# Neighbourhood attention: each score tile as two products of 64 rows instead of one product padded to 128 rows

## The reference, cut to what matters

```python
def neighbourhood_latent(q, k, v, kc, vc, rpb):
    # per grid row r of queries, all heads
    s_loc = einsum('bqhd,bkhd->bhqk', qr, kr) * scale + bias     # 512 latent keys
    s_loc = where(mask, s_loc, -inf)                             # column window of 16
    s_ctx = einsum('bqhd,blhd->bhql', qr, kc) * scale            # 256 context keys
    p = softmax(concatenate([s_loc, s_ctx], -1), -1)
    return p_loc @ vr + p_ctx @ vc

def c_mixer(u, uc, in_w, out_w, rpb):
    q, k, v, z = split(u @ in_w, 4);  q_c, k_c, v_c, z_c = split(uc @ in_w, 4)
    return (neighbourhood_latent(q, k, v, k_c, v_c, rpb) * silu(z)) @ out_w
```

## Time and profile before

| | |
|---|---|
| time, median of 3 runs | 3423.76 us (3420.49 to 3424.57) |
| time of the profiled execution | 3419.06 us |
| its span, first to last instruction | 3417.3 us |
| PE busy | 2899.0 us, 85% |
| DVE, ACT, POOL busy | 833.0, 634.0, 200.3 us |
| mean granted clock of TensorE | 0.939 of full speed |
| attention `na0`, first scores after the bias tables to the next stage's first product | 3004.28 to 3096.57 us |
| attention `na1`, the same | 3276.74 to 3369.75 us |

### The profile page before, as it was taken

One profiled execution on the slowest core, in us unless ns is written; L12 is line 12 of the kernel. 1 busy time (PEld: TensorE's weight loads), 2 busy tenths in 40 slices (PEclk: granted clock), 3 DMA queues, 4 the chain that ended last, 5 costly groups with the idle time before them and its releaser, 6 DMA issues. The chain is left out here.

```text
span 3417.3 us, 30687 instructions
## 1 busy us (share of the span) xinstructions
PE 2899.0 (85%) x12394; PEld 1448.9 (42%) x12394; DVE 833.0 (24%) x2143; ACT 634.0 (19%) x1356; POOL 200.3 (6%) x148
## 2 busy tenths in 40 slices
PE   7999948877768999997688787489999997989987
PEld 3454532222224444444222222256566554455554
DVE  1130421110112212203111101315515351062054
ACT  2220310000001000001000000214414142051043
POOL 1000010000000000000000000200100110021021
PEclk9999969999988999998799999799999998999999
DMA  5502069999984242325699999510010101121010
GB/s 189 220 26 74 25 256 382 411 411 411 411 322 173 98 148 74 117 79 225 259 411 411 411 411 411 214 43 15 1 38 26 39 24 49 54 64 47 28 44 31
DMA packets 191103, 604.84 MB, mean 177 GB/s; under 512 B 9429, under 2 KB 23706, under 8 KB 190826
## 3 DMA queue, kind: packets, MB, share of 16 engines
q1 hardware_dynamic: 165360, 537.15, 40.6%
q10 hardware_dynamic: 20346, 46.88, 4.0%
q0 software_dynamic: 5248, 18.75, 1.5%
HBM read 559.16 MB, written 43.52 MB: 176 GB/s over the span
## 5 line engine op out<-in xcount | busy, mean ns | idle before, releaser
L477 PE MATMUL psum<-ring,XT 128*128 128x512 f32 (+3 forms) x1216 | 480.2, 555 | 14.1 <-ACT arena L1703 6.6
L467 PE MATMUL psum<-XT,ring 128*128 128x512 f32 (+1 forms) x1152 | 444.2, 547 | 2.8 <-DVEq L2053 2.8
L1059 PE MATMUL psum<-arena 128*64 128x512 f32 x1280 | 334.4, 673 | 116.2 <-DMA arena<-in_expert_w_gu 115.9
L477 PEld LDWEIGHTS psum<-ring,XT 128*128 128x128 f32 x1216 | 230.4, 191 | 255.5 <-issue 221.6
L467 PEld LDWEIGHTS psum<-XT,ring 128*128 128x128 f32 x1152 | 219.5, 191 | 226.5 <-issue 215.4
L559 PE MATMUL psum<-ring,arena 128*128 128x512 f32 x704 | 307.8, 596 | 8.5 <-DVEq L2053 4.2
L684 PE MATMUL psum<-arena 128*128 128x512 f32 (+8 forms) x704 | 258.3, 482 | 41.2 <-ACT arena L738 36.1
L1059 PE MATMUL psum<-ring,arena 128*64 128x512 f32 x768 | 199.5, 669 | 75.8 <-DMA ring<-in_expert_w_gu 72.9
L1059 PEld LDWEIGHTS psum<-arena 128*64 128x64 f32 x1280 | 98.7, 153 | 325.5 <-issue 197.8
L1129 DVE TENSOR_TENSOR arena<-arena,psum 64x512 f32<-64x512 f32 x64 | 44.2, 690 | 736.6 <-ACT arena L1132 736.6
L559 PEld LDWEIGHTS psum<-ring,arena 128*128 128x128 f32 x704 | 133.0, 191 | 172.8 <-issue 160.3
(11 more groups left out here) (243 smaller groups left out, 2286.8 us busy)
## 6 DMA issues: line engine op xcount, KB each, us to landing
arena<-in_expert_w_gu SPq DMA_DIRECT2D x80, 2048.0 KB, 25.5
ring<-in_expert_w_gu SPq DMA_DIRECT2D x48, 2048.0 KB, 26.0
arena<-in_expert_w_down SPq DMA_DIRECT2D x40, 2048.0 KB, 24.6
ring<-in_expert_w_down SPq DMA_DIRECT2D x24, 2048.0 KB, 26.0
ring<-in_ada_w SPq DMA_DIRECT2D x12, 2048.0 KB, 8.8
ring<-in_fox_w_in SPq DMA_DIRECT2D x8, 2048.0 KB, 8.3
arena<-xg_dram ACTq DMA_DIRECT2D x32, 512.0 KB, 6.8
y_dram<-arena ACTq DMA_DIRECT2D x128, 128.0 KB, 6.0
```

Of the source, the lines that this page charges most:

```text
L467: i = pe.matmul(ps[0][0:cols_[1] - cols_[0], 0:ntok], w[:, c, cols_[0]:cols_[1]], x[:, c, tok:tok + ntok], start=(c == 0), stop=(c == k - 1))
L477: i = pe.matmul(ps[0][:, 0:width], x[:, c, t * P:(t + 1) * P], w[:, c, c0:c0 + width], start=(c == 0), stop=(c == k - 1))
L1059: i = pe.matmul(psum[side * BR:(side + 1) * BR, 0:FF], x[:, 4 * part + c, :], w[:, c, side * FF:(side + 1) * FF], start=(part == 0 and c = ...
```

## The change

Q is now stored in both halves of the partitions: for each head the same 64 rows stand in partitions 0 to 63 and again in 64 to 127, and no zeros are needed. K is stored per head (`KT` has 8 heads of 384 columns in place of 4 pairs of 768): keys 0 to 383 in partitions 0 to 63, keys 384 to 767 (the last 128 latent keys and the 256 context keys) in partitions 64 to 127. A unit's scores are two products over 64 partitions, each of 384 keys, the one on the upper and the other on the lower half of the array's rows. They write PSUM columns 128 to 511 of the slot's first bank and 0 to 383 of its second, so that each has a bank of its own and the 768 scores are contiguous; all readers are moved by 128 columns (`P`), and the latent part that DVE reads now lies over both banks.

```diff
-                m, x = sm[:, 0, n:n + 1], self.s_at(n, 0, SEQ)
-                dve_step.then(dve, dve.tensor_reduce(m, self.s_at(n, SEQ, SEQ + CTX), AXX, ALU.max))
+                m, x = sm[:, 0, n:n + 1], self.s_at(n, P, P + SEQ)
+                dve_step.then(dve, dve.tensor_reduce(m, self.s_at(n, P + SEQ, P + SEQ + CTX), AXX, ALU.max))
...
-                QT, KT = region(6144, 2, 4, SEQ), region(10240, 4, NTA * P)
+                QT, KT = region(6144, 2, 4, SEQ), region(10240, 8, NTA // 2 * P)
...
-                zeros(p, *(QT[(1 - hh) * DH:(2 - hh) * DH, hh] for hh in range(2)))
...
                         for hh in range(2):
-                            r = slice(hh * DH, (hh + 1) * DH)
-                            i = dve.tensor_scalar(QT[r, hh, n, :], ps[0][r, :], DH ** -0.5, None, ALU.mult)
+                            for half in (slice(0, DH), slice(DH, P)):
+                                i = dve.tensor_scalar(QT[half, hh, n, :], ps[0][hh * DH:(hh + 1) * DH, :], DH ** -0.5, None, ALU.mult)
...
-                    tok_T(p, us[1], 0, KC, 512, (n * P, n * P + P), XT, KT[:, n, :], lambda d: copy_out("a", d), "a", True, n == 3)
+                    def latent_keys(act, ps, n=n, KT=KT):
+                        for hh in range(2):
+                            r = slice(hh * DH, (hh + 1) * DH)
+                            act.activation(KT[0:DH, 2 * n + hh, :], ps[0][r, 0:3 * P], ACT.Copy)
+                            i = act.activation(KT[DH:P, 2 * n + hh, 0:P], ps[0][r, 3 * P:SEQ], ACT.Copy)
+                        return i
+
+                    def context_keys(act, ps, n=n, KT=KT):
+                        for hh in range(2):
+                            i = act.activation(KT[DH:P, 2 * n + hh, P:3 * P], ps[0][hh * DH:(hh + 1) * DH, 0:CTX], ACT.Copy)
+                        return i
+                    p.job("a", mm_T(us[1], 0, KC, 512, (n * P, n * P + P), XT, 0, SEQ), latent_keys, units=(us[1],))
+                    p.job("a", mm_T(us[1], 0, KC, 512, (n * P, n * P + P), XT, SEQ, CTX), context_keys, units=(us[1],),
+                          release=(1,) if n == 3 else ())
...
-                    return [(0, SEQ, q, KT[:, h // 2, 0:SEQ]), (SEQ, SEQ + CTX, q, KT[:, h // 2, SEQ:SEQ + CTX])]
-                a = Neighbours(f"na{g}", 8, NT, lambda i: (0, 768), scores,
+                    return [(P, 4 * P, q[0:DH], KT[0:DH, h, :]), (4 * P, 7 * P, q[DH:P], KT[DH:P, h, :])]
+                a = Neighbours(f"na{g}", 8, NT, lambda i: (P, P + 768), scores,
```

## The result

| | before | after |
|---|---|---|
| time, median of 5 runs | 3423.76 us (3420.49 to 3424.57) | 3404.58 us (3401.82 to 3409.90) |
| ratio, 95% interval | | 0.9945 (0.9934 to 0.9957) |
| profiled execution, its span | 3419.06, 3417.3 us | 3406.55, 3404.8 us |
| na0, first scores to the next stage's first product | 108.29 us | 98.46 us |
| na1, the same | 104.28 us | 93.73 us |

The kernel is 19.2 us faster, 0.55%, where 19 were forecast. The spans of the two profiled executions differ by 12.5 us only, because in the second one everything up to mixer C came 8 us later. The kernel is the same up to there; in the ten traces (the two kernels and the eight experiments) mixer C begins between 2847.3 and 2855.5 us. Of the 8 us, 7 stand already in front of the first expert product (495.5 us before, 502.5 after); their cause was not looked into.

What follows compares the result with a forecast made beforehand. PE (TensorE) bounds both attention stages; 28 pairs x 0.76 = 21.3 us plus 1.8 at the starts, less 3.2 and 0.8, saves 19.1 from 3419.06, giving 3400.0. With 4.7 us to the median: 3405, range 3393 to 3421.

Steps and rivals of the forecast that it cites:

- TensorE bounds both stages: Attention stages na0 and na1: PE is the bound before and after, DVE next at 4.35 us a pair.
- Two row halves take 0.64 us together: A unit's scores: both products of 384 columns overlap fully, 0.64 us in place of 1.29.
- Rival 1: A unit's scores: only the middle records overlap, 0.96 us; a pair takes 5.43, the kernel 3420 us; chance 0.11.
- A change of mode costs 0.18 us: PE between steps of a pair: 5 changes of array tiling in place of 2, giving back 0.54 us a pair.
- Rival 3: Changes of mode to row halves cost nothing; DVE bounds a pair at 4.35 us, the kernel takes 3393; chance 0.08.
- A pair takes 4.79 us: Attention stages, one pair of units: 5.55 us less the overlap plus three changes of mode, 0.76 us less.
- Bias loads cost 0.8 us more each: Twice per attention stage ACT's bias loads delay its exponentials; PE feels 0.8 us more each, 3.2 in all.
- DVE beside POOL, 0.8 us: Attention stages: DVE's line 782 runs longer beside POOL's masks; PE feels 0.8 us for both stages.
- Start of a stage, 0.9 us each: First units of each attention stage: two units' gain is worth nothing, the next two keep 0.9 us per stage.
- I leave the rise of the clock where it is: Start of each attention stage: TensorE's clock was assumed to return from 0.50 to full at the same time as before.
- Projections: nothing: Projection stages: DVE's and ACT's longer copies of Q and K are hidden, POOL's dropped memsets gain nothing.

Runs made afterwards that it cites:

- Experiment 1: Changed kernel with both products of a unit's scores reading the upper 64 partitions, so they can't run beside each other; 3448.46 us, ratio to before 1.0078.
- experiment 7: Changed kernel with each unit's six transposes made on halves of the rows too; 3392.97 us, ratio to before 0.9906.
- Experiment 3: Changed kernel with matmuls without use filling PE's wait for the bias tables in both attention stages; 3403.02 us, ratio to before 0.9935.
- experiment 8: Changed kernel with transposes on row halves and the first four heads' bias tables loaded and masked during the projections; 3378.98 us, ratio 0.9873.

## Why the prediction was right, point by point

- **TensorE bounds both stages.** Right; and it still does, with DVE at 87%.
- **Two row halves take 0.64 us together.** Right, and the term on which all hung. The nearest rows, column halves of an expert stage, told it. Experiment 1 has the other end, 1.28 a pair more. Rival 1 (only the middle overlaps, 0.96) is excluded by the 0.84 from scores to transposes.
- **A change of mode costs 0.18 us.** Measured 0.16 by experiment 1; or, from the pair itself, 4.76 less 2 x 0.64, 2 x 0.65 and 1.29 (the last an estimate, the product with V without a change) leaves 0.89 for five, 0.18. Both are means over several changes. Rival 3 (free) is excluded. That the change of mode is the cause rests on one step of experiment 7, 0.84 to 0.75.
- **A pair takes 4.79 us.** 4.76.
- **Bias loads cost 0.8 us more each.** Too much: a pair with such a load took 5.33 in place of 4.76 us, 0.57 more, where it had been 0.27 before; so 0.3 each and 1.2 in all, not 3.2. I had let nearly all of the lost spare time through. ACT's exponentials are 1.81 us late behind the loads, as before, and PE now feels 0.49 of it in place of 0.20; what took up the rest was not taken apart.
- **DVE beside POOL, 0.8 us.** None was felt: the mean of line 782 in na1 fell from 743 ns to 652 ns, and before, one such stretch in na1 had cost PE 0.65 us. Experiment 3 shows that it could as well have cost 1.3 us per stage. This term hangs on which two instructions meet.
- **Start of a stage, 0.9 us each.** Wrong in its step "I leave the rise of the clock where it is". After the first scores the clock rose 3.0 us later than before in na0 and 2.7 in na1. Units 2 to 6 gained 0.3 and 0.4 us; by the forecast they had to gain 0.9 and a pair's 0.76, 1.66. That is 2.6 us too much for both stages.
- **Projections: nothing.** Right, 140.61 and 138.42 us.

The sizes that were off nearly cancel: the sum had 2.0 (bias loads), 0.8 (POOL), some 0.6 (the stretch in na1) and 28 x 0.03 = 0.8 us (the pair) too little, and 2.6 (the start) too much. It was 19.1 us, the stages show 20.4, the medians 19.2. The pair was understood; that the total agrees to a tenth of a microsecond is luck. The range of 3393 to 3421 us would have held for rivals 1 and 3 as well: it is the pair of 4.76 us and experiment 1 that tell them apart, not the time.

## What to carry to other kernels

Where a product sums over 64 partitions only, zeros in the other 64 cost the full time; two such products on the two halves of the rows, in two PSUM banks, take the time of one. Each alternation with products of another mode cost 0.16 to 0.18 us here on average, so count the changes of mode per loop before: they took back some 40% of what the overlap gave, and putting the transposes on halves of the rows too, where they are faster by themselves, won 5.5 us. A stage's wait at its start may be worth more than its inner loop: loading the tables early gave 21.0 us by the stages (23.5 by the medians) for ten lines.

## What the hardware showed that was not expected

- After an idle stretch the clock of TensorE stayed at its lower level for quite different times, though PE was busy for 96 to 100% of them in na0: 4.9 and 5.5 us with whole products, 7.9 and 8.2 with pairs of halves, 18.6 and 16.6 with one half at a time. The cause is not settled: experiment 7, with both scores and transposes on halves, has 8.0 and 4.2; and in the changed kernel there is an idle gap of 0.35 us between the first two units' scores, and the transposes come earlier. No run took these apart.
- Twelve transposes of 64 x 128 on alternating row halves take 0.51 us to the product with V, six of 128 x 128 0.75, both with products of their own mode in front.
- A division on DVE of 128x768 took 2.48 us in place of 0.62 while POOL added masks in SBUF; the same in the kernel before (2.53) and in experiments 7 (2.53) and 8 (2.52).
- In experiments 7 and 8, where PE is idle for short stretches throughout, its clock fell to the lower level inside na1, once in each.
